# Forgetting attention: the shares are transposed by a product with a diagonal of their reciprocals, in place of a scaling and a product with the identity

## The reference

```
q = (hn @ wq) * (HEAD_DIM_2 ** -0.5)
s = einsum('bhqd,bhkd->bhqk', qb, k)
s = s + fq[..., None] - cum_log_f[:, :, None, :]      # F_t - F_s
s = where(pos_q >= pos_k, s, -inf)
p = softmax(s, axis=-1)
o = einsum('bhqk,bhkd->bhqd', p, v)
return o @ wo
```

## Time and profile before

| | us |
|---|---|
| median of 3 runs | 2145.19 (2143.84 to 2148.71) |
| the profiled execution | 2138.74 |
| its span | 2136.5 |
| mean granted PE clock over the span | 0.982 of full speed |

### The profile page before, as it was taken

The page is one execution under the profiler, slowest core; times in us unless marked ns, Lnnn a source line. Parts: engine busy times, 40 slices in busy tenths (PEclk is TensorE's granted clock), DMA queues, the critical chain, the costliest instruction groups (busy, mean ns, idle before and its releaser), DMA issues.

```text
span 2136.5 us, 31219 instructions
## 1 busy us (share of the span) xinstructions
PE 1984.2 (93%) x10475; PEld 1608.9 (75%) x10475; DVE 1101.3 (52%) x1811; ACT 733.2 (34%) x1233; POOL 1045.8 (49%) x573
## 2 busy tenths in 40 slices
PE   7888998989999999778999999999997799999997
PEld 5677766768887888556778888887876678888886
DVE  6777973754678686688333223132128834122232
ACT  4223234354222322545432222133226643222223
POOL 5466425536865644680554444455453244444442
PEclk9999999999999999889999999999999999999999
DMA  4233002323333333100333333334345423333332
GB/s 144 72 87 105 1 1 71 93 50 89 98 98 90 97 89 91 57 2 1 88 99 94 93 99 94 93 98 103 95 112 124 104 69 91 96 99 98 99 89 89
DMA packets 343417, 179.54 MB, mean 84 GB/s; under 512 B 27950, under 2 KB 335526, under 8 KB 343334
## 3 DMA queue, kind: packets, MB, share of 16 engines
q1 hardware_dynamic: 342592, 177.81, 29.8%
q10 hardware_dynamic: 742, 0.68, 0.1%
HBM read 162.73 MB, written 2.10 MB: 77 GB/s over the span
## 4 chain that ended last, share of the span: by engine, by line
PE 55%; issue 12%; POOL 9%; DVE 9%; POOLq 6%; DVEq 4%; ACT 3%; DMA 2%; SPq 1%; ACTq 0%
PE ACC L1437 16%; PE ACC L1443 15%; PE ACC L1438 15%; POOL WL L1114 7%; POOLq L1124 2%; DVEq L2226 1%; POOLq L1296 1%; POOLq L1284 1%; DVE PTL L2232 1%; ACT WH L551 1%; DMA RAW<-in_w_v_cross_dram 1%; PE O L1559 1%; PE ST L1559 1%; PE ACC L1596 1%; PE ST L1561 1%
## 5 line engine op out<-in xcount | busy, mean ns | idle before, releaser
L1114 POOL TENSOR_TENSOR WL<-RAW,WH 128x1024 fp32r<-128x1024 f32 (+1 forms) x308 | 733.4, 2383 | 779.6 <-ACT WH L551 712.6
L1437 PE MATMUL ACC<-PH,WH 128*128 128x512 f32 x1248 | 493.9, 396 | 12.6 <-DVE PL L1966 3.6
L1438 PE MATMUL ACC<-PL,WH 128*128 128x512 f32 x1248 | 487.9, 391 | 0.0
L551 ACT ACTIVATE WH<-RAW 128x1024 fp32r<-128x1024 f32 (+1 forms) x308 | 317.6, 1033 | 492.9 <-PE ACC L1443 408.8
L1437 PE MATMUL ACC<-QH,WH 128*128 128x512 f32 (+1 forms) x1136 | 431.0, 384 | 20.7 <-ACT WH L551 15.2
L1438 PE MATMUL ACC<-QL,WH 128*128 128x512 f32 (+1 forms) x1136 | 426.1, 379 | 0.0
L1443 PE MATMUL ACC<-PH,WL 128*128 128x512 f32 x1248 | 311.1, 391 | 0.0
L1437 PEld LDWEIGHTS ACC<-PH,WH 128*128 128x128 f32 x1248 | 235.6, 189 | 71.7 <-DVE PL L1966 4.9
L1443 PE MATMUL ACC<-QH,WL 128*128 128x512 f32 (+1 forms) x1136 | 272.6, 381 | 10.8 <-POOL WL L1114 10.7
L1443 PEld LDWEIGHTS ACC<-PH,WL 128*128 128x128 f32 x1248 | 234.0, 188 | 52.6 <-issue 3.3
L1438 PEld LDWEIGHTS ACC<-PL,WH 128*128 128x128 f32 x1248 | 235.5, 189 | 48.9 <-issue 1.0
(11 more groups left out here) (418 smaller groups left out, 2440.9 us busy)
## 6 DMA issues: line engine op xcount, KB each, us to landing
RAW<-in_mlp_w_dram SPq DMA_DIRECT2D x128, 512.0 KB, 4.1
RAW<-in_w_gate_dram SPq DMA_DIRECT2D x22, 512.0 KB, 3.8
RAW<-in_w_up_dram SPq DMA_DIRECT2D x22, 512.0 KB, 3.8
RAW<-in_w_in_dram SPq DMA_DIRECT2D x16, 512.0 KB, 3.8
RAW<-in_w_down_dram SPq DMA_DIRECT2D x16, 512.0 KB, 4.1
RAW<-in_ssm_w_glu_dram SPq DMA_DIRECT2D x16, 512.0 KB, 3.9
RAW<-in_w_kvf_dram SPq DMA_DIRECT2D x16, 512.0 KB, 4.0
RAW<-in_w_k_cross_dram SPq DMA_DIRECT2D x8, 512.0 KB, 4.2
```

The lines of the kernel that those rows point to most:

```text
L551: act.activation(WH[:, s, 0:kc], RAW[:, s, 0:kc], ACT.Copy).then_inc(w_hi, 1)
L1114: pool.tensor_tensor(WL[:, s, 0:kc], RAW[:, s, 0:kc], WH[:, s, 0:kc], ALU.subtract).then_inc(w_lo, 1)
L1437: pe.matmul(ACC[s][:, 0:n], WH[:, s, k, :], xh[:, k, :], start=(k == 0), stop=False)
L1438: pe.matmul(ACC[s][:, 0:n], WH[:, s, k, :], xl[:, k, :], start=False, stop=False)
```

## The change

For the fox tiles, divide makes only the reciprocal and raises a new semaphore, rec_ready. ACT makes DGS, the identity with row i multiplied by REC of row i, in a new step scaled(n), which stands first at tile n of its list; it raises e_scaled. turn multiplies the unscaled E4 block (as weights) with DGS as a full float32 product, in place of a transposition of the scaled block. DGS has two slots. The sparse and cross tiles keep the scaling and the identity. VS, angc, normed_x and q_lo were not used.

```
+        DGS = at("DGS", [P, 2, P], F32, 184320)
...
-        e_scaled = sem("e_scaled")
+        e_scaled, rec_ready = sem("e_scaled"), sem("rec_ready")
...
+            def scaled(kind, n, t):
+                nk, j = keys(kind, t), t % SLOTS[kind]
+                act.wait_ge(rec_ready, n + 1)
+                act.activation(DGS[:, t % 2, :], IDENT, ACT.Copy, scale=REC[:, j, :]).then_inc(e_scaled, 1)
...
                 for n in range(64):
                     c, t = divmod(n, 8)
+                    scaled("fox", TILES["fox"] + n, t)
                     if n + 2 < 64:
                         exponentials("fox", TILES["fox"] + n + 2, t + 2)
                     turned_high("fox", c, t)
...
                 for k in range(keys(kind, t) // P):
-                    mm = pe.transpose(TT[t % 2][:, k * P:(k + 1) * P], E4[kind][slot(kind, c, t)][:, k * P:(k + 1) * P], IDENT)
+                    block = E4[kind][slot(kind, c, t)][:, k * P:(k + 1) * P]
+                    if kind == "fox":
+                        mm = pe.matmul(TT[t % 2][:, k * P:(k + 1) * P], block, DGS[:, t % 2, :], start=True, stop=True)
+                    else:
+                        mm = pe.transpose(TT[t % 2][:, k * P:(k + 1) * P], block, IDENT)
...
-                dve.reciprocal(REC[:, j, :], SUM[:, j, :])
-                dve.drain()
-                dve.tensor_scalar(E4[kind][j][:, 0:nk], E4[kind][j][:, 0:nk], REC[:, j, :], None, ALU.mult).then_inc(e_scaled, 1)
+                dve.reciprocal(REC[:, j, :], SUM[:, j, :]).then_inc(rec_ready, 1)
+                if kind != "fox":
+                    dve.drain()
+                    dve.tensor_scalar(E4[kind][j][:, 0:nk], E4[kind][j][:, 0:nk], REC[:, j, :], None, ALU.mult)\
+                       .then_inc(e_scaled, 1)
```

More of the change, by code:

```diff
@@ L335, in build_program @@
             sem(n) for n in ("mem_sq", "mem_var", "mem_std", "mem_scaled", "mem_t", "mem_hi", "mem_lo"))
-        pos_in, ang, angc, tables = sem("pos_in"), sem("ang"), sem("angc"), sem("tables")
+        pos_in, ang, tables = sem("pos_in"), sem("ang"), sem("tables")
         u_zero, gate_raw, gate_sig = sem("u_zero"), sem("gate_raw"), sem("gate_sig")
@@ L356, in build_program @@
         rho_used, powers, w_made, c_made, cleared = (sem(n) for n in ("rho_used", "powers", "w_made", "c_made", "cleared"))
-        normed_x, un_ready, uc_ready = sem("normed_x"), sem("un_ready"), sem("uc_ready")
+        un_ready, uc_ready = sem("un_ready"), sem("uc_ready")
         glu_out = sem("glu_out")
@@ L367, in build_program @@
         q_hi = sem("q_hi")
-        q_lo = sem("q_lo")
         s_ready = sem("s_ready")
```

## The result

| | before | changed |
|---|---|---|
| median (lowest to highest), us | 2146.17 (2143.84 to 2148.71), 4 runs | 2172.98 (2172.25 to 2178.01), 4 runs |
| profiled execution, us (its span) | 2138.74 (2136.5) | 2172.87 (2170.7) |
| first turn to last PTH copy, us | 115.96 | 150.88 |

The medians lie 26.8 us apart. The ratio of the runs is 1.0134 (95% interval 1.0114 to 1.0153), which is 24.5 to 33 us. The forecast was 2178 in a range of 2160 to 2204, with 0.90 for slower. The time fell inside the range, 5 us under the forecast.

The account below looks back on a forecast made before the run. DVE's queue was taken to set the fox stage's pace, replaced after the change by a PE-ACT ring: +29.3 us plus 4 for clock, sum +33, so 2172 for the profiled execution and 2178 median, range 2160 to 2204.

Parts of the forecast that it names:

- The mechanism: Fox attention stage: PE's next turn waits for ACT's diagonal, queued behind the PTH copy that waits for PE's values; +29.3 us.
- DVE's relief: DVE loses 64 drains and scalings, some 4 to 5 us a pair, worth time only if nothing else becomes the pace.
- the ring: Fox stage: turn, values on PE, PTH copy, diagonal on ACT, next turn; 19.0 us a pair against 14.5.
- The longest step: Within each pair, tile t4, with both splits ahead of the diagonal on ACT: 3.18 us.
- The diagonal: ACT's 64 products of identity with REC: 0.30 us each plus 0.06 for the release of PE, together 0.36.
- The products: PE's turn: 0.22 us a 128-column block against 0.11 for a transposition; over 160 blocks 17.6 us of PE time.
- a factor of four: Rival, PE's turn: a product at four times a transposition's price, upper bound 0.43 a block, 34 us more, 2212; chance 0.03.
- The first pair: Start of the fox stage: no values, wait or out_high in its first half, so 16.2 us in all.
- the clock term: Fox stage: PE's low-clock share of some 12% kept, costing 5 us or none; taken as +4 us.
- Faster: Rival: the ring does not bind and DVE's relief shows until PE is the pace; 10 us gained, 2135; chance 0.05.
- level: Rival: the ring does not bind, with 4.5 of the 19 us a pair hidden; 2145; chance 0.05.
- Low clock: Rival: half to all of the stage at 1.2 GHz, ring pays 23 to 66 us; 2197 to 2240; chance 0.09.

Follow-up runs that it names:

- e1: Changed kernel with ACT making the next tile's diagonal ahead of the PTH copy instead of behind it; 2153.10 us, ratio 1.0036 to the kernel before.
- f1: Changed kernel with ACT making the next tile's diagonal first thing and DVE its reciprocal ahead of the PTL subtraction; 2140.31 us.
- f2: Changed kernel with the diagonal made by DVE, where the scaling was, and ACT's list as before; 2142.98 us.
- e4: Changed kernel with DVE also keeping its drain and a scaling of E4 by one, which turn waits for; 2173.13 us.
- e2: Changed kernel with turn again a transposition by the identity, still waiting for DGS, blocks left unscaled; 2164.14 us.
- f3: Kernel before, scaling kept, with each fox block turned by a full float32 product with the identity; 2143.59 us.
- g3: Changed kernel profiled again, unedited; 2175.47 us.
- The repeats: Kernel before profiled again twice and changed kernel once, all unedited; 2140.31, 2149.64 and 2175.47 us.
- f4: Changed kernel with DVE making both reciprocal and diagonal of the next tile one tile early; 2152.12 us.
- e3: Changed kernel with the next diagonal right behind the PTH copy, ahead of out_high, splits and values_high; 2163.03 us.
- g5: Changed kernel with ACT making each diagonal twice, the first into a buffer that nothing reads; 2192.2 us, one execution.

## Why the prediction was right, point by point

**The mechanism held.** PE waits for ACT's diagonal at 62 tiles, and taking the diagonal out from behind the PTH copy takes most of the loss (e1) or all of it (f1, with DVE's order) away, as does taking it off ACT (f2). e4 shows that DVE's relief is worth nothing. In the stage the 34.9 us are the ring, 17.6 without the products (e2), and 17.4 more for the products inside it. These aren't two separate prices: without the ring the same products cost 0 to 3 us (f3).

**The ring, tile by tile.** A full pair was predicted at 19.0 us and took 19.1 (windows, pair 1), the one without splits 18.1 against 18.0, the last 16.7 against 16.6. The longest step is t = 4 with both splits, as predicted: it ran from 1634.16 to 1637.31, 3.15 us against 3.18.

**The diagonal** was under-priced in one way. The term was 0.30 and 0.06 for the release; from its start to PE's turn it is 0.45 (1740.62 to 1741.07; 0.44 at 1742.68). Its group among the groups by form of the changed kernel (count, busy us, mean ns), and the copy beside it:

```profile
L692 ACT ACTIVATE DGS<-CST,REC 128x128 f32<-128x128 f32 x62 | 24.5, 395 | 0.0
...
L703 ACT ACTIVATE PTH<-ACC 128x128 fp32r<-128x128 f32 x15 | 4.2, 278 | 7.9 <-PE O L1567 7.9
```

The 0.09 us too few were made good by the steps before it: from turn to values 0.44 at t = 0, where 0.53 was counted, and 0.70 at t = 2 (1743.12 to 1743.82), where 0.76 was. Two small errors cancelled; at t = 3, which has no values in it, the 0.11 stayed (2.14 against 2.03).

**The products.** 0.22 us a block, 0.11 over the transposition: as predicted from the run of eight in the earlier trace rows, by the durations and by e2. The Trainium skill (TensorE: Matmul & The Clock Gate, section Terms) states a factor of four for float32, which as an estimate would have made it 0.44 a block and another 35 us. The trace disagrees for blocks of 128 columns, where the factor is two (0.22 against 0.11 us).

**The first pair** is the term that was wrong: 20.4 us (6.55 and 13.88) against 16.2. Its first half was near, 6.55 against 6.19. In the second half PE waits before the scores of the next pair. The timeline of the changed kernel there:

```profile
1610.93 2.72 SPq L516 DMA_DIRECT2D R<-RF  x4
...
1615.63 0.45 PE L1592 MATMUL FOUR<-R,L 128*128 128x128 f32 x1 [2.52 <-ACT E3fox L686]
...
1619.25 1.65 PE L1604 MATMUL ACC<-DGS,E2fox 128*128 128x128 f32 x6 [0.29 <-ACT DGS L692]
```

ACT's E3fox is named, but its last record had ended at 1615.04. The code makes these scores wait for the transfers R<-RF too (bias_in). SP issued the last of the four at 1613.1, and they took 2.4 to 2.5 us to land, so until about 1615.6. In the repeat g3 the last was issued at 1615.1 and the scores began at 1617.71, in f1 at 1612.8 and 1615.36. The times fit these transfers as the release in all three; an earlier issue of them was not tried. The kernel before has the same wait at nearly the same time:

```profile
1615.46 0.30 PE L1586 MATMUL FOUR<-R,L 128*128 128x128 f32 x1 [1.52 <-issue]
```

So the wait was to be seen, and the table left it out. Around it the granted clock is low. The windows of the changed kernel at t = 4, 5 and 6 of pair 0:

```profile
1611.27:1616.30 5.03, 2.51 (x12) 1.98 (x13) 1.41 (x5) 2.79 (x8) 2.49 (x2) 0.86 0.61 141
1616.30:1619.25 2.95, 2.66 (x12) 2.47 (x12) 0.60 (x2) 0.73 (x3) 2.07 (x2) 0.50 0.58 133
1619.25:1623.02 3.77, 3.17 (x16) 2.97 (x16) 1.37 (x5) 1.68 (x7) 0.00 (x0) 0.67 0.89 207
```

At 0.50 PE is at 1.2 GHz, and the six products of 1619.25 take 1.65 us where they take 0.94 in pair 7. The step with the wait is 1.9 us over its 3.18, and the two behind it are together 1.9 over their 2.07 and 2.76. So the low clock cost about 1.9 us, in one place, where the clock term had 4, spread over the stage. That 4 also made up for the wait, which had no term, and for the 0.1 and 0.5 us by which other steps were under-priced. That is luck.

**The sum.** 34.9 us of stage against 29.3 + 4, and a profiled execution of 2172.87 against 2172 forecast for its like. Small slips in the working: t = 2 of the first half is 1.72 by its terms, not 1.70; the wait from the turn's end to the copy is 0.26 by the earlier trace rows (0.70 less four steps of 0.11), not 0.21, though the changed kernel comes nearer to the latter (1745.83 to 1747.03 is 1.20, less 0.98 for the turn); and the first turn came 0.05 us earlier (1604.72 against 1604.77), not 0.5. The step that was mis-sized most is the last: the 6.5 us by which the median of before lies over its profiled execution were added for the changed kernel too, whose median is 0.1 over its own. The repeats show why. The profiled execution of before was one of its faster ones, and others took up to 2149.64, with a granted clock of 0.91 in the stage and a later start of it. For the same reason the medians give 27 us where the profiled executions give 34.

The mean granted clocks of all executions add to this. The kernel before has a median of 0.979 in the 44 executions measured beside e1 to f4 (0.974 to 0.983), and e2, which also transposes, 0.977 to 0.979 in its four. The kernels that turn by products (the changed one, e1, e3, e4 and f1 to f4) have 0.982 in 59 executions (0.976 to 0.986). f3 differs from the kernel before in the products alone, and has 0.983 in ten. So the kernels that transpose here do run at the lower granted clock, and part of what the products cost may come back that way in the medians. Why the clock differs is open, and so is how much of the time it accounts for.

**The rivals.** Faster and level fell with the stage, 34.9 us longer, and the waits for the diagonal. Low clock: the stage has 0.98, more than before's 0.94, and 0.96 in the repeat, so half of the stage at 1.2 GHz is out. That the idle pieces of 0.5 to 1.3 us never bring the clock down isn't shown. In the profiled execution the one fall came during the wait of 2.5 us, but g3 fell again at 1660 to 1663 and g5 at 1693 to 1699, with no wait of PE over 1.0 us in the 6 us ahead of either. Of what the prediction said would show it, the activation's 0.28 to 0.32 us was wrong (0.395); the rest was there: stage 150.9 in 140 to 155, PE's wait 36.8 over 25, DVE at 46% under 60.

## What to carry to other kernels

When work moves to another engine's queue, write down what stands ahead of it there and what that waits for: if the chain comes back to the engine that will wait for the moved work, a ring is closed, and every step in it counts at full length, however idle the engines are. Price it link by link, start to start. And before giving such a change up, try the early place on every engine in the ring: one early step (e1) gave back 20 of 27 us, both (f1) all of it, and the same work in another queue (f2) all of it too. An early place can also stall the engine it is on (f4), so measure it.

## What the runs showed of the hardware that I had not expected

- ACT's copy of 128 x 128 from SBUF with a scale for each partition lasts 0.395 us, the plain copy from PSUM 0.278. Its queue pays less: the next activation starts 0.29 us after it (1742.68 to 1742.97; 0.17 after the plain copy, 1740.45 to 1740.62), and a second one for each tile adds 0.25 (g5). The reader of its result pays the long figure, 0.45 from start to turn; the queue pays the short one.
- At full clock a full float32 product of 128 columns costs 0.22 us, in the ring (x8 in 1.16 us) and outside it (x8 in 1.10 us in f1), and a transposition 0.11 (x4 in 0.66 us in e2); but what the products cost the stage was 0 to 3 us in f3 and 17.4 in the ring.
- The same program's stage ran at a granted clock of 0.94, 0.94 and 0.91, and its time outside the stage was 2020.5, 2022.9 and 2028.7 us, with nothing changed.
